# Attention norms in batches of four, and both log-gate products in one step

## The reference, cut to what matters

```python
h = rms_norm(x, norm_mix)
proj = h @ w_in                       # 512 tokens; fq, fk, fv, ff, gq, gk, gv, gr, glr, sz, sxbc, sdt, gates
q = rms_norm(fq by heads of 64, q_gain) * 64 ** -0.5
k = rms_norm(fk by heads of 64, k_gain)
c = cumsum(log_sigmoid(ff + fox_f_bias))              # one column per head
sc = q @ k.T + c[:, None] - c[None, :]; p = softmax(causal sc); o = p @ v
log_a = log_sigmoid(glr @ gla_w_lr + gla_b_gate) / 16 # the log gates of gla, rank 16
bcum = cumsum(log_a) inside chunks of 64 tokens
```

## Time and profile before

| | us |
|---|---|
| median of 3 runs | 951.37 |
| lowest and highest run | 950.45, 953.74 |
| span of the profiled execution (first to last instruction) | 948.3 |
| TensorE busy (PE) | 855.5 |
| VectorE busy | 573.2 |
| ScalarE busy | 486.4 |
| GpSimd busy | 109.9 |

### The profile page before, as it was taken

The page is one execution under the profiler, slowest core; times in us unless marked ns, Lnnn a source line. Parts: engine busy times, 40 slices in busy tenths (PEclk is TensorE's granted clock), DMA queues, the critical chain, the costliest instruction groups (busy, mean ns, idle before and its releaser), DMA issues.

```text
span 948.3 us, 11203 instructions
## 1 busy us (share of the span) xinstructions
PE 855.5 (90%) x4072; PEld 675.7 (71%) x4072; DVE 573.2 (60%) x643; ACT 486.4 (51%) x564; POOL 109.9 (12%) x107
## 2 busy tenths in 40 slices
PE   2998799999999888999999999639999999998993
PEld 2766666777876666788888888238888888876772
DVE  5644336874544776433254253657998998987880
ACT  5366835553453422222232222218888888867870
POOL 5400000000000110100000010010422322322010
PEclk9999999999997999999999999859999999999997
DMA  6331111222112110233322567757999999999991
GB/s 209 108 102 44 43 47 46 89 89 90 46 45 80 54 46 17 72 98 112 102 89 89 177 221 270 279 208 272 364 359 372 369 359 372 368 359 373 371 302 31
DMA packets 85177, 169.38 MB, mean 179 GB/s; under 512 B 8761, under 2 KB 9874, under 8 KB 85138
## 3 DMA queue, kind: packets, MB, share of 16 engines
q1 hardware_dynamic: 76080, 145.89, 43.4%
q0 software_dynamic: 4896, 17.83, 7.2%
q10 hardware_dynamic: 4162, 5.13, 1.6%
HBM read 155.21 MB, written 13.63 MB: 178 GB/s over the span
## 4 chain that ended last, share of the span: by engine, by line
PE 56%; DMA 17%; DVE 10%; ACT 7%; issue 5%; POOL 0%; DVEq 0%; SPq 0%; ACTq 0%; POOLq 0%
PE bank L1724 16%; PE bank L1725 16%; PE bank L1726 16%; DMA mstage<-in_w_exp_down 7%; DMA mstage<-in_w_exp_up 6%; DMA mstage<-in_w_exp_gate 4%; ACT whi L646 1%; DVE wlo L659 1%; PE bank L1828 1%; DVE stt L1369 1%; PE bank L1859 1%; PE bank L2041 1%; PE bank L1844 1%; ACT L998 1%; PE bank L2107 1%
## 5 line engine op out<-in xcount | busy, mean ns | idle before, releaser
L659 DVE TENSOR_TENSOR wlo<-mstage,whi 128x2048 fp32r<-128x2048 f32 x96 | 218.5, 2290 | 41.3 <-ACT whi L646 40.5
L646 ACT ACTIVATE whi<-mstage 128x2048 fp32r<-128x2048 f32 x96 | 184.1, 1917 | 48.6 <-PE bank L1726 32.7
L659 DVE TENSOR_TENSOR wlo<-stage,whi 128x2048 fp32r<-128x2048 f32 (+1 forms) x40 | 90.8, 2273 | 127.4 <-ACT whi L646 127.0
L1724 PE MATMUL bank<-hTh,whi 128*128 128x512 f32 x368 | 150.9, 410 | 1.7 <-DVE foxq L1317 1.7
L1726 PE MATMUL bank<-hTh,wlo 128*128 128x512 f32 x368 | 145.4, 395 | 0.0
L1725 PE MATMUL bank<-hTl,whi 128*128 128x512 f32 x368 | 145.4, 395 | 0.0
L646 ACT ACTIVATE whi<-stage 128x2048 fp32r<-128x2048 f32 (+1 forms) x40 | 74.9, 1873 | 89.2 <-PE bank L1726 83.4
L1724 PE MATMUL bank<-whi,xTh 128*128 128x512 f32 x256 | 104.3, 407 | 2.4 <-DVE xTl L1666 1.6
L1726 PE MATMUL bank<-whi,xTl 128*128 128x512 f32 x256 | 101.1, 395 | 0.0
L1725 PE MATMUL bank<-wlo,xTh 128*128 128x512 f32 x256 | 100.9, 394 | 0.0
L1724 PEld LDWEIGHTS bank<-hTh,whi 128*128 128x128 f32 x368 | 70.4, 191 | 19.5 <-issue 3.4
(11 more groups left out here) (368 smaller groups left out, 1327.9 us busy)
## 6 DMA issues: line engine op xcount, KB each, us to landing
mstage<-in_w_exp_gate SPq DMA_DIRECT2D x32, 1024.0 KB, 12.3
mstage<-in_w_exp_up SPq DMA_DIRECT2D x32, 1024.0 KB, 13.5
mstage<-in_w_exp_down SPq DMA_DIRECT2D x32, 1024.0 KB, 12.1
stage<-in_w_in SPq DMA_DIRECT2D x28, 1024.0 KB, 5.0
stage<-in_w_branch SPq DMA_DIRECT2D x6, 1024.0 KB, 5.0
stage<-in_w_out SPq DMA_DIRECT2D x4, 1024.0 KB, 5.2
xin<-in_x SPq DMA_DIRECT2D x4, 512.0 KB, 5.3
x<-in_x SPq DMA_DIRECT2D x4, 512.0 KB, 7.2
```

Of the source, the lines that this page charges most:

```text
L646: nc.scalar.activation(whi[:, s, :, 0:n], source_of(u)[:, :, 0:n], ACT.Copy).then_inc(hi_ready, 1)
L659: nc.vector.tensor_tensor(wlo[:, s, :, 0:n], source_of(u)[:, :, 0:n], whi[:, s, :, 0:n].bitcast(F32), ALU.subtract).then_inc(lo_ready, 1)
L1724: t.matmul(out, lhs[0], rhs[0], start=start, stop=False)
```

## The change

Three things are done, all within the first 125 us:

1. The gates of gla. Both products of "loga" are made one after the other, behind part 1 of fq's first unit. Their biased values go to one tile (lgz), and one Abs and one Exp cover both. Ln of the small columns moves from "small" to a new item "logs" behind part 3, where Ln of both gates (one instruction) follows it. The minimum, factor and scans of both gates are a new item "bcum" on VectorE alone, behind part 0 of fk's second unit. "lo 2" moves behind part 2.
2. The norms. The square of part m stands right behind its piece, "qnorm m" (product and Ln) behind the next one. Behind qnorm 3 and qnorm 7 stand two "root" items (one Exp over two parts each), and then the four scalings ("qscale"). qrs has four parts in place of two and lies elsewhere.
3. "tokrows" moves from fv to the end of fk's first unit, and scores 0 and 1 move one part ahead: behind part 0 and part 2 of fv's second unit.

```diff
@@ -90,19 +90,24 @@
     last = [p for p in pieces if p[1] >= NB - 2]
 
     out = [("small",)]
-    early = {(0, 0, 3): [("loga", 0)], (1, 1, 1): [("loga", 1)], (2, 0, 2): [("tokrows",)]}
-    waiting = [[], [], [], []]
-    ahead = {(2, 1, 1): 0, (2, 1, 3): 1}
+    early = {(0, 0, 1): [("loga",)], (0, 0, 2): [("lo", 2)], (0, 0, 3): [("logs",)], (1, 0, 3): [("tokrows",)],
+             (1, 1, 0): [("bcum",)]}
+    waiting = [[], []]
+    ahead = {(2, 1, 0): 0, (2, 1, 2): 1}
     for p in first:
         out.append(p)
         if p[3] == 0 and p[4] == 0:
-            out += [("hi", 2 * p[1] + p[2] + 2), ("lo", 2 * p[1] + p[2] + 2)]
+            u = 2 * p[1] + p[2] + 2
+            out += [("hi", u)] if u == 2 else [("hi", u), ("lo", u)]
         if p[4] == 1:
             out += early.get(p[1:4], [])
-        if p[4] == 1:
             out += waiting[0]
             m = [4 * p[1] + p[3]] if p[1] < 2 and p[2] == 1 else []
-            waiting = [[("square", q) for q in m] + waiting[1], waiting[2], waiting[3], [("qnorm", q) for q in m]]
+            out += [("square", q) for q in m]
+            done = [("qnorm", q) for q in m]
+            if m and m[0] % 4 == 3:
+                done += [("root", m[0] - 3), ("root", m[0] - 1)] + [("qscale", q) for q in range(m[0] - 3, m[0] + 1)]
+            waiting = [waiting[1], done]
             if p[1:4] in ahead:
                 n = ahead[p[1:4]]
                 out += [("score", n)] + [(kind, n, hh) for kind in ("exp", "norm") for hh in range(2)]
@@ -207,7 +212,8 @@
         if kind == "small":
             uses[4].append("small")
         elif kind == "loga":
-            uses[5 + it[1]].append(it)
+            uses[5].append(("loga", 0))
+            uses[6].append(("loga", 1))
         elif kind == "tokrows":
             uses[7].append(it)
         elif kind == "piece" and it[2] == 0 and it[4] == 0:
@@ -418,7 +424,9 @@
         sme = at("sme", 148, [P, T])
         fv = at("fv", Z0 + 12, [P, NT, MIX])
         qsq = at("qsq", Z0, [P, 2, T])
-        qrs = at("qrs", Z0 + 4, [P, 2, T])
+        qrs = at("qrs", 136, [P, 4, T])
+        lgz = at("lgz", 120, [P, 2, T])
+        lge = at("lge", 124, [P, 2, T])
         cum16 = at("cum16", 128, [16, T])
         prob = at("prob", Z0, [P, 2, 2, T])
         probT = at("probT", 144, [P, 2, 2, T])
@@ -946,18 +954,18 @@
                     act.wait_ge(z_done, 1)
                     step(a.activation(sme[0:16, :], smz[0:16, :], ACT.Abs))
                     step(a.activation(sme[0:16, :], sme[0:16, :], ACT.Exp, scale=-1.0))
+                elif kind == "loga":
+                    for pr in range(2):
+                        act.wait_ge(free[5 + pr], turn(5 + pr, ("loga", pr)) + 1)
+                    step(a.activation(lge[:, :, :], lgz[:, :, :], ACT.Abs))
+                    step(a.activation(lge[:, :, :], lge[:, :, :], ACT.Exp, scale=-1.0))
+                elif kind == "logs":
                     step(a.activation(sme[0:16, :], sme[0:16, :], ACT.Ln, bias=1.0), lnv_done, 1)
+                    step(a.activation(lge[:, :, :], lge[:, :, :], ACT.Ln, bias=1.0), lnv_done, 2)
                     act.wait_ge(rows_done, 1)
                     act.wait_ge(sel_done, 1)
                     for q in range(2):
                         step(a.activation(cumhl[64 * q:64 * q + 16, :], cum16[:, :], ACT.Copy), cumh_done, q + 1)
-                elif kind == "loga":
-                    pr = it[1]
-                    act.wait_ge(free[5 + pr], turn(5 + pr, it) + 1)
-                    act.wait_ge(rows_done, 1 + pr)
-                    step(a.activation(sme[:, :], smz[:, :], ACT.Abs))
-                    step(a.activation(sme[:, :], sme[:, :], ACT.Exp, scale=-1.0))
-                    step(a.activation(sme[:, :], sme[:, :], ACT.Ln, bias=1.0), lnv_done, 2 + pr)
                 elif kind == "tokrows":
                     act.wait_ge(toktr_done, 1)
                     step(a.activation(eacs[:, :, :], tokrow[:, :, 24:32], ACT.Exp), eacs_done, 1)
@@ -993,10 +1001,13 @@
                     m = it[1]
                     b = 4 + m % 2
                     act.wait_ge(full[b], turn(b, it) + 1)
-                    if m >= 2:
-                        act.wait_ge(qn_done, m - 1)
-                    step(a.activation(qrs[:, m % 2, :], whole(b), ACT.Ln, bias=epsc[:, 0:1]), free[b], turn(b, it) + 1)
-                    step(a.activation(qrs[:, m % 2, :], qrs[:, m % 2, :], ACT.Exp, scale=-0.5), qrs_done, m + 1)
+                    if m >= 4:
+                        act.wait_ge(qn_done, m - 3)
+                    step(a.activation(qrs[:, m % 4, :], whole(b), ACT.Ln, bias=epsc[:, 0:1]), free[b], turn(b, it) + 1)
+                elif kind == "root":
+                    m = it[1]
+                    step(a.activation(qrs[:, m % 4:m % 4 + 2, :], qrs[:, m % 4:m % 4 + 2, :], ACT.Exp, scale=-0.5),
+                         qrs_done, m // 2 + 1)
                 elif kind == "exp":
                     _, n, hh = it
                     w = (n % NT + 1) * P
@@ -1256,11 +1267,6 @@
                                             in1=hTh[:, k, :].bitcast(F32), op0=ALU.mult, op1=ALU.subtract),
                      free[k], turn(k, "hT") + 1)
 
-            def logsig(z, e, n):
-
-                dve.wait_ge(lnv_done, n)
-                step(v.scalar_tensor_tensor(out=z, in0=z, scalar=0.0, in1=e, op0=ALU.min, op1=ALU.subtract))
-
             def per_head(ap):
 
                 return ap.unsqueeze(2).to_broadcast([P, SSM_H, 64])
@@ -1279,6 +1285,13 @@
                     step(v.tensor_scalar(smz[0:16, :], bank[4][0:16, :], bias16[:, 0:1], sgn16[:, 0:1], ALU.add, ALU.mult),
                          z_done, 1)
                     step(v.tensor_copy(sm[32:48, :], bank[4][32:48, :]), free[4], turn(4, "small") + 1)
+                elif kind == "loga":
+                    for pr in range(2):
+                        b = 5 + pr
+                        dve.wait_ge(full[b], turn(b, ("loga", pr)) + 1)
+                        step(v.tensor_scalar(lgz[:, pr, :], whole(b), cols[:, R_GB + pr:R_GB + pr + 1], None, ALU.add),
+                             free[b], turn(b, ("loga", pr)) + 1)
+                elif kind == "logs":
                     dve.wait_ge(lnv_done, 1)
                     step(v.scalar_tensor_tensor(out=sm[0:16, :], in0=smz[0:16, :], scalar=0.0, in1=sme[0:16, :],
                                                 op0=ALU.min, op1=ALU.subtract))
@@ -1290,16 +1303,14 @@
                         dve.wait_ge(cumh_done, q + 1)
                         step(v.tensor_tensor(cumhl[64 * q + 32:64 * q + 48, :], cum16[:, :],
                                              cumhl[0:16, :].bitcast(F32), ALU.subtract), cuml_done, q + 1)
-                elif kind == "loga":
-                    pr = it[1]
-                    b = 5 + pr
-                    dve.wait_ge(full[b], turn(b, it) + 1)
-                    step(v.tensor_scalar(smz[:, :], whole(b), cols[:, R_GB + pr:R_GB + pr + 1], None, ALU.add),
-                         free[b], turn(b, it) + 1)
-                    logsig(smz[:, :], sme[:, :], 2 + pr)
-                    step(v.tensor_scalar(smz[:, :], smz[:, :], 1.0 / 16.0, None, ALU.mult))
-                    step(v.tensor_tensor_scan(bcum[:, pr, :], reset64[:, :], smz[:, :], 0.0, ALU.mult, ALU.add),
-                         rows_done, 2 + pr)
+                elif kind == "bcum":
+                    dve.wait_ge(lnv_done, 2)
+                    step(v.scalar_tensor_tensor(out=lgz[:, :, :], in0=lgz[:, :, :], scalar=0.0, in1=lge[:, :, :],
+                                                op0=ALU.min, op1=ALU.subtract))
+                    step(v.tensor_scalar(lgz[:, :, :], lgz[:, :, :], 1.0 / 16.0, None, ALU.mult))
+                    for pr in range(2):
+                        step(v.tensor_tensor_scan(bcum[:, pr, :], reset64[:, :], lgz[:, pr, :], 0.0, ALU.mult, ALU.add),
+                             rows_done, 2 + pr)
                 elif kind == "tokrows":
                     dve.wait_ge(full[7], turn(7, it) + 1)
                     step(v.tensor_copy(tokrow[:, :, :], bank[7][:, 0:128].rearrange("p (i c) -> p i c", c=32)),
@@ -1320,12 +1331,12 @@
                         dve.wait_ge(tanh_done, tanhs)
                         step(v.scalar_tensor_tensor(out=(grs if name == "gr" else zs)[:, s, :], in0=tnhb[:, :], scalar=1.0,
                                                     in1=whole(s), op0=ALU.add, op1=ALU.mult), free[s], n)
-                elif kind == "qnorm":
+                elif kind == "qscale":
                     m = it[1]
-                    dve.wait_ge(qrs_done, m + 1)
+                    dve.wait_ge(qrs_done, m // 2 + 1)
                     q = (foxq if m < 4 else foxk)[:, m % 4, :]
                     gain = gain1[:, 1:2] if m < 4 else cols[:, R_FK:R_FK + 1]
-                    step(v.scalar_tensor_tensor(out=q, in0=q, scalar=gain, in1=qrs[:, m % 2, :],
```

(9 more changed lines are left out.)

## The result

The changed kernel takes 935.16 us (median of 4 runs, 934.13 to 942.09) against 952.3 us (4 runs) for the kernel before: ratio 0.9848, 95% interval [0.9822, 0.9875]. Two later sets of the same kernel gave 935.39 us (0.9821 [0.9791, 0.9852]) and 937.58 us (0.9854 [0.9819, 0.9888]). Over all 14 runs the median is 935.4 and the mean 937.0 us; 43 runs of the kernel before have a mean of 951.8 us. The forecast was 940.2, range 936.8 to 945.0: right direction, right stops, and a gain (11.2 us) that was too small by some 3 to 5 us. The first set lies 1.6 us outside the range by its median. By the ratios, taken from the 951.37 us of the forecast, the three sets stand at 936.9, 934.3 and 937.5 us: two just inside the fast edge of the range, one outside.

What follows compares the result with a forecast made beforehand. TensorE was taken as the bound, with holes: 15.6 us lost, less 4.1 for a new stop and 0.4 for a small one, gives 11.1, taken as 11.2 off 951.37: 940.2 us, range 936.8 to 945.0.

Steps and rivals of the forecast that it cites:

- The stops that go: Five TensorE stops between 50 and 125 us: 11.4 us idle plus 0.8 us of edges, all to go.
- The new stop at qnorm 0: TensorE waits for the square in block fq: 2.2 us idle, 4.1 us with edge and clock fall.
- The small stop at qnorm 5: In block fk, the square behind "bcum" comes late: 0.3 to 0.4 us, no clock fall.
- The slack before score 0: Last scaling ends at 99.5 us, score 0 stands at 101.5: 2 us of slack, no stop.
- Table loads: ScalarE's function-set loads fall from 18 to four; 14 x 1.28 = 17.9 us of ScalarE time go.
- rival 4: Late chain of weight loads gives the gain back if something there is fixed in time: 951.4 us; chance 0.07.
- The time without the clock: Up to the scores: stops and edges removed, less the new stops, 12.2 - 2.4 - 0.4 = 9.4 us gained.
- The clock: TensorE's granted clock: 3.4 us of falls behind two old stops go, 1.7 us comes behind the new one.
- Rival 1: At qnorm 0, no clock fall or no GpSimd delay of wlo 3: 938.5 to 937.0 us; chance 0.20.
- (2): A second full stop on a square in block fk, 4.3 us: 944.5 us; chance 0.17.
- (3): Six table loads of block fk stay, stopping TensorE 5.7 us at score 0: 947.7 us; chance 0.02.
- (5): TensorE stops at the squares, 4.3 us each; six such stops give 961.6 us, slower; chance 0.04.

Runs made afterwards that it cites:

- GpSimd held back: Changed kernel with GpSimd's acsw and acsm waiting until wlo of unit 4 is done; median 935.7 us, ratio 0.9831.
- the shifted ones: Changed kernel with one or two idle 1.06 us ScalarE copies ahead of the hTh copies, meant to move everything later; 938.0 and 939.2 us.
- the scores at their old places: Changed kernel with scores 0 and 1 back behind parts 1 and 3 of fv's second unit; median 940.3 us, ratio 0.9869.
- the loads brought back: Changed kernel with a one-column Exp, result unused, behind each of the norms' eight logarithms; median 946.2 us, ratio 0.9960.
- the shifted kernel before: Kernel before the change with one idle 1.06 us ScalarE copy ahead of the hTh copies, meant to move everything later; 952.3 us.

## Why the prediction was right or wrong, point by point

**The stops that go** (the term of 11.4 us idle and 0.8 us of edges). Right, all five.

**The new stop at qnorm 0.** Right in place, cause and length: 2.2 us forecast, 2.19 measured; wlo 3 at 3.65 forecast, 3.66 measured, shown by the run with GpSimd held back. The timetable holds as a whole: score 2 was forecast at 111.8 us with a fall behind this stop, and the one profile that has the fall shows 111.97.

**The small stop at qnorm 5**, 0.3 to 0.4 us forecast: 0.30. **The slack before score 0**, 2 us forecast: the last scaling ended at 98.4, score 0 was at 100.2, 1.8 us. **Table loads**, four forecast: four (of the three that the prediction gives to the gate logarithms before, one stands ahead of the first gate's Exp, L959; the 18 hold). **Nothing given back behind**: in the first profile TensorE's steps behind score 2 moved by 12.6 us or more, the last hid transpose from 926.8 to 911.0, which settles rival 4.

**The time without the clock.** Mean span less clock loss is 911.0 us before and 902.1 after: 8.9 us. The forecast's terms without the clock are 12.2 - 2.4 - 0.4 = 9.4, which is right within the scatter.

**The clock: the term that was mis-sized.** I put it at 3.4 - 1.7 = 1.7 us; it is 38.7 - 32.5 = 6.2 us over the 14 runs (standard error 1.0), 5.5 with the shifted ones (0.7). Two errors are in it. First, I took a fall behind the 2.2 us stop as certain, because one had followed the stop of 2.4 us and another one of 2.2 us at 319 us; seven profiles have that stop at qnorm 0 (those of the changed kernel and its shifted versions, the scores at their old places, the loads brought back), and one of the seven has a fall. Rival 1 was the case of the first profile, and its 938.5, the figure with GpSimd's delay, which the runs confirm, is nearer to the measured times than my 940.2. A fall is not decided by the length of a stop alone: the 1.65 us stop before score 2 was followed by one in two of four profiles, 2.2 us was not in six of seven, 2.0 us brought three falls in one execution and none in another. It should have stood as an expected value. Second, I gave each of the two stops that go one fall, as in the one profile that I had; the shifted kernel before has four falls from 88 to 130 us in its profile, not two: one behind the 2.5 us stop, two behind the 4.8 us one and one behind the 1.65 us one. Three falls for the stops that go, the mean of these two profiles, less a seventh of one for the new stop, make 4.9 us, an estimate that the measured 5.5 to 6.2 us agree with. Whether the place of the later stops in time has a part in the rest stays open: the runs meant to tell it moved nothing. This term is what made the forecast gain too small: it was 4 to 4.5 us short, while the terms without the clock were 0.5 us too high.

**The rivals.** (2), a second full stop in block fk, didn't come. (3), the loads stay, is what the kernel with loads brought back tries: 946.2 us by its median, 947.7 forecast. That the two are so near is luck: it has twelve loads back, not six, a stop of 4.0 us before score 0 in place of 5.7, and stops at the squares, which I had not priced. (5), a stop at each square, is not there with the gates merged; with the gates left as they were one of 5.1 us stands alone. So the norm part needs the gate part, which the forecast did not say.

## What to carry to other kernels

Count the function changes in ScalarE's order, not its functions: twelve loads of 1.28 us brought back into a chain that TensorE waits for cost 10 to 11 us, while ScalarE itself is half idle. But time saved ahead of a wait that a slow chain sets is given back at that wait (the gates alone), and work pulled ahead asks for its inputs ahead too (the norms alone): walk each queue by the durations of the trace before deciding the order. And give the clock as a spread: here a stop of 2.0 us cost its idle time plus zero, three or four times 1.7 us. What decides it these runs don't show, so one profile can't price a short stop.

## What the runs showed of the hardware that was not expected

The granted clock can fall behind an idle time of 1.65 us (0.57 over the window 113 to 117 us, scores at their old places) and need not fall behind 2.2 us (1.00 over 53.4 to 57 us). The clock loss has a standard deviation of 2.0 us over 43 runs of the kernel before and of 3.5 us over 14 of the changed one, whose times have 3.3 us: there it is the largest part of the scatter, and 14 runs give a mean with a standard error of 0.9 us. A GpSimd product of 64x1024 from SBUF lengthens a VectorE subtraction of 128x2048 with both inputs in SBUF by 1.37 us where they overlap by some 1.5 us (2.29 and 3.66 us); a VectorE copy of 128x512 out of PSUM beside the same product is not lengthened (0.69 us).
